# Depthwise convolution with 128-column stationaries and streams, and sample projections in four column quarters

## The chip, the cores and the metric

The kernel runs on one core of one Trainium2 chip. A core has TensorE (PE; its loads of stationary operands are PEld), VectorE (DVE), ScalarE (ACT), GpSimd (POOL), and SyncE (SP), which here issues most DMAs. Each runs its own list of instructions in order, and they meet at semaphores. The metric is the device time of one execution in microseconds (us). All data is float32. In the trace each float32 matmul shows as two records, and each transpose as one.

## The reference, cut to what matters

One decoder layer for 2048 prompt tokens and 8 sample tokens (one new token of each of 8 sequences). A projection of width 1792 is split into attention (512 query, 128 key, 128 value columns) and a convolution branch (512 value and 512 gate columns):

```python
proj = einsum('btd,de->bte', x, w_in) + b_in
q, k, v, ca, cg = split(proj)
attn = windowed attention (128 keys) of q, k, v with sinks
u = ca * sigmoid(cg)
conv = silu(layer_norm(depthwise_causal_conv(u, conv_w) + conv_b))    # width 31, 512 channels
mix = concat([attn, conv]) @ w_out + b_out
h = layer_norm(ALPHA * x + mix)
y = layer_norm(ALPHA * h + hierarchical_moe(h))                       # 32 experts, top 2
```

## The kernel before

The program is staged as follows, with the times of the profile.

**Input of the convolution (to 217 us).** The 16 prompt tiles of 128 tokens (`CONV_IN`) are projected onto the 1024 columns of the convolution branch, most of them in pairs (`pair_in`), and last the sample (`sample_in`, tile `NT`). DVE adds the biases (`evict_pair`, `evict_in`), ACT takes the sigmoid, DVE multiplies (`gated_in`), and SP stores `u` to DRAM (`u_rows`). `gather_windows(t)` then loads the stored rows back as overlapping windows into `ug`: partitions hold 62 positions of each of two channel quarters (plus two rows of ones for the bias), and the free axis holds 64 windows by 256 channels, so that the 64 windows of one channel lie 256 elements apart. SP works through its list in order; the load of the next x tile (`load_xT(18)`, which waits for `sample_in`) stands ahead of the last `gather_windows`.

**Attention and convolution (217 to 579 us), `STEPS` = 19 steps.** `QKV_IN` has the sample first. In step s, PE projects q, k, v of tile s (`project_sample` in step 0, else `project_in` with line 740: 512 query columns, then 256 key and value columns), and does the scores, transposes (`flip`) and values of tile s - 2. The order inside a step is written out by hand: first part of a convolution chunk, transposes of q and k (`turn_qk`, lines 756 and 757), second value half, scores (line 762), projection of q, (sample's own attention pieces in steps 1 to 9), projection of k and v, `flip` of the first half (line 770), second part of the chunk, `values` of the first half (line 778), `flip` of the second half. `values` waits for ACT's copy of the first flip (`ptA_ev`, line 1204), and `turn_qk` of the next step for ACT's copy of the second flip (`ptB_ev`, line 1213).

The convolution is done as Toeplitz products in 16 chunks (`CHUNK_OF`: two in step 0, two in step 1, then one a step up to step 13). A chunk is 8 slots by 2 column halves; each matmul (line 793) has 126 partitions, a stationary of 64 columns (two channels by 32 positions) and a stream of the 64 windows. The halves `h` = 0 and 1 go to output partitions 0 to 63 and 64 to 127 of the one bank `M1`, and one ACT copy (line 1209) moves the chunk's 128 x 512 results to `conv_sb`. The tables `toe` have two buffers; SP loads the table of chunk c + 2 after chunk c is done (`load_toe`, line 433), in its list behind the load of x for step s + 2, which waits for the key and value projection of step s. When all chunks are done, `conv_sb` goes to DRAM.

The sample's rows are few (8), so its projections (`sample_in`, lines 694 and 695; `project_sample`, line 747; `project_out_sample`, line 861) use 8-column stationaries and put two column halves into output partitions 0 to 7 and 64 to 71 (`rows_at`), with streams of 512 (384 for q, k, v). DVE adds bias or x from those partitions; line 1346 is the last add of `evict_in`, which PE waits for ahead of step 0.

**Output projection, h, routing (579 to 890 us); experts (to 1320 us); final norm.** In step 17 `project_out_sample` stands between the scores and the first flip of the last tile. The first prompt tile's output projection (`project_out(1, 0)`, line 874) waits for DVE's add of the sample's result (line 1496), which needs x plus bias from POOL (`bias_x`, line 1883) after POOL has scaled the bias (line 1902). The sample's x is loaded by `load_x(0)` in step 17, ahead of `load_attn(1)` and `load_attn(2)` on SP.

## Time and profile before

| | |
|---|---|
| median of 3 runs | 1383.74 us (1380.58 to 1384.69) |
| the profiled execution's own time | 1386.9 us |
| its span, first to last instruction | 1385.0 us |
| PE busy | 1276.4 us (92%) |
| DVE, ACT, POOL busy | 734.4, 539.4, 472.4 us |
| mean granted PE clock | 0.971 of full speed |

PE's busy time is long, but the ends of its records are modelled and records overlap; the starts are what to read. An entry in square brackets in a timeline is idle time of the engine ahead of the row and what ended it. A row that covers several instructions (x16) gives the start of the first and the length up to the end of the last.

### The profile page before, as it was taken

The page shows a single profiled execution, that of the slowest core. Times are in us where ns is not written, and L with a number is a line of the kernel's source. Part 1 is how long each engine was busy: PE and PEld are TensorE (multiplying, and loading weights), DVE is VectorE, ACT ScalarE, POOL GpSimd, SP SyncE. Part 2 cuts the span into 40 slices and gives each one's busy share as a digit, 9 for nine tenths or more (in the row PEclk, how much of TensorE's full clock was granted, in tenths as well). Part 3 has the DMA queues.
Part 4 walks back from the last instruction along what each step waited for, and adds up shares of the span by engine and source line. Part 5 has one row for each costly group of instructions (what it writes and reads, how often), then busy time and mean ns, then how long its engine had stood idle before and what let it go on. Part 6 is the DMA issues. An engine that isn't in the chain of part 4 may idle for free.

```text
span 1385.0 us, 21099 instructions
## 1 busy us (share of the span) xinstructions
PE 1276.4 (92%) x5477; PEld 607.3 (44%) x5478; DVE 734.4 (53%) x2079; ACT 539.4 (39%) x881; POOL 472.4 (34%) x640
## 2 busy tenths in 40 slices
PE   8999999989999988799999999999999999999910
PEld 3434444657666655355545555433333333333300
DVE  2423333463655555568888997344444444444338
ACT  0000101333445343323333331266665666656544
POOL 5112210000000000355555563344666566666312
PEclk9999999999999999999999999999999999999965
DMA  6354533222112165256655552269989999999776
GB/s 260 106 198 157 178 119 111 77 92 77 65 50 77 61 208 165 89 210 225 220 199 178 166 153 77 72 183 318 318 261 369 355 283 316 332 365 368 208 245 277
DMA packets 89957, 269.70 MB, mean 195 GB/s; under 512 B 14496, under 2 KB 40672, under 8 KB 76742
## 3 DMA queue, kind: packets, MB, share of 16 engines
q1 hardware_dynamic: 72903, 223.90, 45.2%
q0 software_dynamic: 14144, 41.26, 12.4%
q10 hardware_dynamic: 2823, 3.54, 0.8%
q8 instruction: 35, 0.57, 0.2%
q14 instruction: 52, 0.43, 0.1%
HBM read 209.66 MB, written 63.25 MB: 197 GB/s over the span
## 4 chain that ended last, share of the span: by engine, by line
PE 49%; issue 29%; DVE 9%; DMA 5%; DVEq 4%; ACT 1%; POOL 1%; SPq 1%; POOLq 1%; ACTq 0%
PE P L1032 13%; PE bank_S L1054 10%; PE M L1032 6%; PE bank_S L701 4%; PE P L701 3%; PE bank_T L701 2%; PE P L904 2%; PE bank_S L874 2%; DMA work<-conv_rows 2%; DVEq L1577 2%; PE M L701 2%; DVE route L1582 1%; PE M L1040 1%; DMA big<-sum_rows 1%; DVE work L1539 1%
## 5 line engine op out<-in xcount | busy, mean ns | idle before, releaser
L1272 ACT ACTIVATE big<-big 128x2048 f32 x78 | 148.9, 1910 | 155.4 <-issue 113.3
L1032 PE MATMUL P<-big,work 128*64 x416 | 188.0, 595 | 1.8 <-DVE work L1759 1.6
L1033 PE MATMUL P<-big,work 128*64 128x512 f32 x416 | 188.0, 595 | 0.0
L740 PE MATMUL P<-big,work 128*128 128x256 f32 (+1 forms) x512 | 173.6, 496 | 0.0
L1928 POOL DMA_INDIRECT work<-h_rows,piece_idx x152 | 145.8, 959 | 72.1 <-issue 51.4
L1054 PE MATMUL bank_S<-big,work 128*64 x312 | 140.4, 593 | 2.5 <-issue 1.5
L1056 PE MATMUL bank_S<-big,work 128*64 128x512 f32 x312 | 140.4, 593 | 0.0
L1865 POOL TENSOR_SCALAR work<-work 128x1 f32<-128x1 f32 (+1 forms) x17 | 3.8, 221 | 376.7 <-DVE work L1465 376.7
L740 PEld LDWEIGHTS P<-big,work 128*128 128x128 f32 x512 | 97.3, 194 | 70.4 <-issue 63.6
L874 PE MATMUL P<-big,work 128*128 128x512 f32 x256 | 113.8, 597 | 3.5 <-DVE work L1496 3.5
L874 PE MATMUL bank_S<-big,work 128*128 128x512 f32 x256 | 115.5, 605 | 0.0
L1032 PEld LDWEIGHTS P<-big,work 128*64 128x64 f32 x416 | 54.8, 137 | 108.7 <-issue 105.8
L1032 PE MATMUL M<-big,work 128*64 x208 | 94.2, 595 | 0.0
L1033 PE MATMUL M<-big,work 128*64 128x512 f32 x208 | 94.2, 595 | 0.0
L1746 DVE COPY work<-M 128x256 f32<-128x256 f32 x39 | 16.6, 425 | 125.3 <-PE M L1040 96.8
L1054 PEld LDWEIGHTS bank_S<-big,work 128*64 128x64 f32 x312 | 42.5, 137 | 91.7 <-issue 91.6
L1278 ACT ACTIVATE big<-big 128x2048 f32 x39 | 74.4, 1907 | 14.3 <-issue 13.7
L1101 ACT ACTIVATE work<-work 128x512 f32<-128x512 f32 (+1 forms) x17 | 10.7, 630 | 176.5 <-DVE work L1365 134.5
L1113 ACT ACTIVATE work<-work 128x256 f32<-128x256 f32 x128 | 63.4, 496 | 40.4 <-DVE work L1402 40.4
L1733 DVE STREAM_TRANSPOSE work<-work 128x1024 f32<-128x1024 f32 x38 | 77.7, 2045 | 0.3 <-issue 0.2
L874 PEld LDWEIGHTS P<-big,work 128*128 128x128 f32 x256 | 47.4, 190 | 57.3 <-issue 53.6
L874 PEld LDWEIGHTS bank_S<-big,work 128*128 128x128 f32 x256 | 48.0, 192 | 54.8 <-issue 54.7
(310 smaller groups left out, 2274.6 us busy)
## 6 DMA issues: line engine op xcount, KB each, us to landing
big<-in_w SPq DMA_DIRECT2D x96, 1024.0 KB
work<-in_xt_prompt SPq DMA_DIRECT2D x32, 512.0 KB, 3.5
big<-sum_rows SPq DMA_DIRECT2D x16, 520.0 KB, 8.9
big<-in_toe SPq DMA_DIRECT2D x16, 512.0 KB, 3.3
work<-in_x_prompt SPq DMA_DIRECT2D x16, 512.0 KB, 4.0
h_rows<-work SPq DMA_DIRECT2D x16, 512.0 KB
sum_rows<-work SPq DMA_DIRECT2D x16, 512.0 KB
out_y_prompt<-big SPq DMA_DIRECT2D x16, 512.0 KB
```

The costliest lines, as they stand in the source:

```text
L701: last = mm(dst, lhs[:, k, :], rhs[:, k, :], start=(first and k == 0), stop=(final and k == KD // 2 - 1), skip_group_check=not first)
L740: last = mm(dst[0:n, 0:c1 - c0], lhs[:, k, :], w_qkv[:, k, c0:c1], start=(k == 0), stop=(k == KD - 1))
L874: last = mm(OUT[c][half][0:n, :], lhs[:, k, :], w_out[:, k, half * 512:(half + 1) * 512], start=(k == 0), stop=(k == KD - 1))
L1032: mm(lower, xgT[j][:, k, 0:U], both[:, k], start=(k == 0), stop=(k == KD - 1))
L1033: last = mm(upper, xgT[j][:, k, U:P], w_up[:, k], start=(k == 0), stop=(k == KD - 1))
L1054: mm(bank_S[0:U, cols], gT[:, k, 0:U], wmem[:, bass.ds(off + 2 * KD * FF + k * D + half * 512, 512)], start=(k == 0), stop=(k == 1))
L1056: last = mm(bank_S[U:P, cols], gT[:, k, U:P], w_dn[side][:, k, cols], start=(k == 0), stop=(k == 1))
L1113: fn(smx[:, i, :], smx[:, i, :], ACT.Exp, bias=nm[:, c0 + i:c0 + i + 1], scale=SCALE, accum_out=rs[:, c0 + i:c0 + i + 1])
L1272: fn(w_up.rearrange("p k m f -> p m k f")[:, :, ks, :], src, ACT.Copy).then_inc(s[f"wu{part}_ok"], 1)
L1278: fn(dn_copy[b % 2], wmem[:, bass.ds(off + 2 * KD * FF, 2 * D)], ACT.Copy).then_inc(s["wd_ok"], 1)
L1733: nc.vector.transpose(xgT[j].rearrange("p k (i t) -> p i k t", i=4), xg[j].rearrange("p (i f k) -> p i k f", i=4, k=KD)).then_inc(s["xgT_e ...
L1928: g.indirect_dma_start(xg[j][:, 256 * i:256 * (i + 1)], None, h_pieces, bass.IndirectOffsetOnAxis(ap=piece_idx[:, j, i // 2, i % 2:i % 2 + ...
```

## The change

Four things change together.

1. The convolution's matmuls take both column halves at once: stationary of 128 columns (`h`, channel, position), stream of 128 columns (`h`, window). Half of the 128 x 128 output is used. Eight matmuls a chunk take the place of sixteen. Half a chunk (4 matmuls, `conv_part(chunk, part)`) now fills a bank of 512 columns; the first four half chunks go to four different banks (`CONV_FIRST`), all later ones to `M1`.
2. ACT evicts half a chunk at a time (`evict_conv`), in two copies of 64 partitions by 256 elements; `pe_cv` and `cv_ev` count half chunks.
3. The order in steps 0 and 1 differs: in step 1 the first part of chunk 2 stands ahead of the query projection, its second part behind it, the first part of chunk 3 behind the sample's piece, its second part at the end.
4. The sample's three projections use four column quarters at output partitions 0, 32, 64 and 96 (`quarter_rows`), with streams of 256 (192 for q, k, v), and DVE's adds and the load of the sample's x are split accordingly.

```diff
@@ helpers
+        ug_pairs = ug.rearrange("p w (h n) -> p h w n", h=2)
+        CONV_FIRST = [M1[:, :], bank_S[:, 0:512], bank_S[:, 512:], bank_T[:, 0:512]]
+        def conv_bank(n):
+            return CONV_FIRST[n] if n < len(CONV_FIRST) else M1[:, :]
-        def rows_at(tile, side):
-            at = side * HD if tile == NT else 0
-            return slice(at, at + rows_of(tile))
+        def quarter_rows(q):
+            return slice(32 * q, 32 * q + DEC)
@@ SP
             def load_toe(chunk):
-                after(sp, s["pe_cv"], chunk - 2)
+                after(sp, s["pe_cv"], chunk - 2, per=2)
...
                 if tile == NT:
-                    for half in range(2):
-                        cols = slice(512 * half, 512 * (half + 1))
-                        sp.dma_start(xb[0][rows_at(NT, half), cols], a["x_sample"][:, cols]).then_inc(s["xr_in0"], 16)
+                    for q in range(4):
+                        cols = slice(256 * q, 256 * (q + 1))
+                        sp.dma_start(xb[0][quarter_rows(q), cols], a["x_sample"][:, cols]).then_inc(s["xr_in0"], 16)
@@ PE: sample_in
-                    mm(CA[0][0:n, :], lhs[:, k, :], (B11 if low else B21)[:, kk, :], start=(k == 0), stop=(k == KD - 1))
-                    last = mm(CG[0][rows_at(NT, 1), :], (x_neg if low else x_sum)[:, kk, :], (T3 if low else B22)[:, kk, :],
-                              start=(k == 0), stop=(k == KD - 1))
+                    value = (lhs[:, k, :], (B11 if low else B21)[:, kk, :])
+                    gate = ((x_neg if low else x_sum)[:, kk, :], (T3 if low else B22)[:, kk, :])
+                    for q in range(4):
+                        bank, (tokens, weights) = ((CA[0], value), (CG[0], gate))[q // 2]
+                        cols = slice(256 * (q % 2), 256 * (q % 2 + 1))
+                        last = mm(bank[quarter_rows(q), cols], tokens, weights[:, cols], start=(k == 0), stop=(k == KD - 1))
@@ PE: project_sample (project_out_sample likewise, with 256 columns of w_out)
-                    for side, bank in enumerate((P0, P1)):
-                        last = mm(bank[rows_at(NT, side), 0:QKV // 2], lhs[:, k, :],
-                                  w_qkv[:, k, side * QKV // 2:(side + 1) * QKV // 2], start=(k == 0), stop=(k == KD - 1))
+                    for q in range(4):
+                        last = mm((P0, P1)[q // 2][quarter_rows(q), 0:QKV // 4], lhs[:, k, :],
+                                  w_qkv[:, k, q * QKV // 4:(q + 1) * QKV // 4], start=(k == 0), stop=(k == KD - 1))
@@ PE: the convolution
             def conv_part(chunk, part):
+                n = 2 * chunk + part
+                if n == 0:
+                    pe.wait_ge(s["ug_in"], 16 * 4 * NT)
                 if part == 0:
-                    if chunk == 0:
-                        pe.wait_ge(s["ug_in"], 16 * 4 * NT)
-                        after(pe, s["c_ev"], NT)
                     pe.wait_ge(s[f"toe_in{chunk % 2}"], 16 * (chunk // 2 + 1))
-                    after(pe, s["cv_ev"], chunk - 1)
-                for slot in range(4 * part, 4 * part + 4):
-                    for h in range(2):
-                        channel = h * P + chunk * 8 + slot
-                        last = mm(M1[h * 64:(h + 1) * 64, slot * 64:(slot + 1) * 64],
-                                  toe[chunk % 2][0:2 * SPAN + 2, slot, h, :], ug[0:2 * SPAN + 2, :, channel],
-                                  start=True, stop=True)
-                if part == 1:
-                    last.then_inc(s["pe_cv"], 1)
+                if n >= len(CONV_FIRST):
+                    after(pe, s["cv_ev"], n - 1)
+                for i in range(4):
+                    slot = 4 * part + i
+                    last = mm(conv_bank(n)[:, i * P:(i + 1) * P], toe[chunk % 2][0:2 * SPAN + 2, slot].rearrange("p h m -> p (h m)"),
+                              ug_pairs[0:2 * SPAN + 2, :, :, chunk * 8 + slot], start=True, stop=True)
+                last.then_inc(s["pe_cv"], 1)
@@ PE: order in the step loop
                 elif I:
                     pe.wait_ge(*x_landed(load))
                     after(pe, s["q_ev"], step - 1)
+                    if step == 1:
+                        conv_part(chunks[0], 0)
                     project_in(P0, load, 0, AD, s["pe_q"])
+                    if step == 1:
+                        conv_part(chunks[0], 1)
...
                 if step == 1:
-                    conv_part(chunks[0], 0)
-                    conv_part(chunks[0], 1)
+                    conv_part(chunks[1], 0)
...
-                if step <= 1:
+                if step == 0:
                     conv_part(chunks[1], 0)
+                    conv_part(chunks[1], 1)
+                elif step == 1:
                     conv_part(chunks[1], 1)
@@ ACT
+            def evict_conv(n):
+                at = n // 2 * 8 + n % 2 * 4
+                after(act, s["pe_cv"], n)
+                for h in range(2):
+                    rows = slice(64 * h, 64 * (h + 1))
+                    got = conv_bank(n)[rows, :].rearrange("p (n h w) -> p w h n", n=4, h=2)[:, :, h, :]
+                    last = fn(conv_sb[rows, :, at:at + 4], got, ACT.Copy)
+                last.then_inc(s["cv_ev"], 1)
...
+                if step >= 2 and CHUNK_OF[step]:
+                    evict_conv(2 * CHUNK_OF[step][0])
...
-                for chunk in CHUNK_OF[step]:
-                    after(act, s["pe_cv"], chunk)
-                    fn(conv_sb[:, :, chunk * 8:chunk * 8 + 8], M1[:, :].rearrange("p (j w) -> p w j", j=8),
-                       ACT.Copy).then_inc(s["cv_ev"], 1)
+                if step == 0:
+                    for n in range(4):
+                        evict_conv(n)
+                elif step == 1:
+                    evict_conv(2 * CHUNK_OF[1][1])
+                    evict_conv(2 * CHUNK_OF[1][1] + 1)
+                elif CHUNK_OF[step]:
+                    evict_conv(2 * CHUNK_OF[step][0] + 1)
@@ DVE: the sample's first add (those of q, k, v and of the output projection likewise)
+            def evict_sample():
+                b = NT % 2
+                after(v, s["pe_x"], NT)
+                for q in (2, 3):
+                    rows, cols = quarter_rows(q), slice(256 * (q - 2), 256 * (q - 1))
+                    tt(cgb[b][0:DEC, cols], CG[b][rows, cols], b_conv[rows, 256 * q:256 * (q + 1)], ALU.add)
+                after(v, s["u_st"], NT - 2, per=16)
+                for q in (0, 1):
+                    rows, cols = quarter_rows(q), slice(256 * q, 256 * (q + 1))
+                    last = tt(u[b][0:DEC, cols], CA[b][rows, cols], b_conv[rows, cols], ALU.add)
+                last.then_inc(s["c_ev"], 1)
```

## Rows read from the trace of the kernel before

**Rows 1.** Windows, 257 to 500 us: busy us (count) by engine, granted clock, DMA

```profile
257.00:500.00 243.00, 237.38 (x1416) 155.96 (x1415) 129.72 (x546) 105.00 (x298) 1.46 (x4) 0.99 0.20 68
```

**Rows 2.** Instructions of lines 694 and 695: ns min/median/max, first and last start

```profile
L694 PE MATMUL P<-big,work x16: 592/592/597, 210.6 to 217.0; 128*8 128x512 f32 x16
...
L695 PE MATMUL P<-big,smp x16: 592/592/596, 210.6 to 217.0; 128*8 128x512 f32 x16
```

**Rows 3.** Timeline, 357 to 363 us: start, length, engine, line, shape

```profile
357.73 1.36 PE L793 MATMUL M<-big 126*64 126x64 f32 x16
357.83 1.07 ACT L1204 ACTIVATE work<-bank_T 128x1024 f32<-128x1024 f32 x1 [3.74 <-PE bank_T L770]
...
358.96 1.08 PE L778 MATMUL M<-work 128*64 128x256 f32 x8
...
359.97 1.09 PE L770 MATMUL bank_S<-const,work 128*128 128x128 f32 x8
...
361.10 1.03 ACT L1213 ACTIVATE work<-bank_S 128x1024 f32<-128x1024 f32 x1 [1.36 <-PE bank_S L770]
...
362.28 0.65 PE L756 MATMUL bank_S<-const,work 128*128 128x128 f32 x4
```

**Rows 4.** Timeline, 557 us, a step without convolution work

```profile
557.40 1.08 PE L778 MATMUL M<-work 128*64 128x256 f32 x8 [1.12 <-ACT work L1204]
```

**Rows 5.** Timeline of PE at 238 us and at 596 us

```profile
238.23 0.41 PE L807 MATMUL M<-const,work 8*128 8x8 f32 x4
238.50 0.39 PE L809 MATMUL M<-const,work 8*128 8x8 f32 x4
...
596.11 1.04 PE L883 MATMUL bank_T<-const,work 8*128 8x8 f32 x8
597.08 0.70 PE L874 MATMUL bank_S<-big,work 128*128 128x512 f32 x1
```

**Rows 6.** Timeline, 214 to 231 us, with the DMA queue of SP

```profile
214.58 0.39 SPq L477 DMA_DIRECT2D u_rows<-work  x1
...
219.27 5.33 PE L747 MATMUL P<-big,work 128*8 128x384 f32 x32 [1.68 <-DVE work L1346]
219.41 0.44 SPq L428 DMA_DIRECT2D big<-u_rows  x1
...
224.53 2.55 PE L793 MATMUL M<-big 126*64 126x64 f32 x32
...
230.30 7.13 PE L740 MATMUL P<-big,work 128*128 128x512 f32 x16
```

**Rows 7.** DMA issues, 195 to 240 us: KB each, median us to landing

```profile
big<-in_toe SPq DMA_DIRECT2D x4, 512.0 KB, 3.3
...
big<-u_rows SPq DMA_DIRECT2D x6, 120.0 KB, 3.8
u_rows<-work SPq DMA_DIRECT2D x2, 256.0 KB, 2.4
```

**Rows 8.** Timeline of PE, 245 to 251 us

```profile
245.96 2.53 PE L793 MATMUL M<-big 126*64 126x64 f32 x32
250.99 1.22 PE L793 MATMUL M<-big 126*64 126x64 f32 x14 [2.50 <-DMA big<-in_toe]
```

**Rows 9.** Timeline of PE at 309 us, and window from 309 to 314.5 us

```profile
308.93 0.34 PE L831 MATMUL M<-const,smp 64*128 64x64 f32 x1 [3.74 <-DVE smp L1454]
...
309.00:314.50 5.50, 5.50 (x14) 4.30 (x15) 1.25 (x5) 0.22 (x1) 0.00 (x0) 0.50 0.00 0
```

**Rows 10.** Timeline, 568 to 580 us, the last attention step

```profile
568.53 1.14 DVE L1412 TENSOR_SCALAR work<-work 128x256 f32<-128x256 f32 x4
...
571.29 1.09 PE L770 MATMUL bank_T<-const,work 128*128 128x128 f32 x8
...
574.64 2.35 POOL L1883 TENSOR_TENSOR work<-work,lnx 128x1024 f32<-128x1024 f32 x1
...
579.11 7.13 PE L874 MATMUL P<-big,work 128*128 128x512 f32 x16 [3.50 <-DVE work L1496]
```

More of the change, by code:

```diff
@@ L859, in project_out_sample @@
                 for k in range(KD):
-                    for half in range(2):
-                        last = mm(OUT[c][half][rows_at(NT, half), :], mix_sT[:, k, :], w_out[:, k, half * 512:(half + 1) * 512],
+                    for q in range(4):
+                        at = 256 * (q % 2)
+                        last = mm(OUT[c][q // 2][quarter_rows(q), at:at + 256], mix_sT[:, k, :], w_out[:, k, 256 * q:256 * (q + 1)],
                                   start=(k == 0), stop=(k == KD - 1))
@@ L964, in _ @@
                 if step == NT + 1:
-                    after(pe, s["cv_ev"], CHUNKS - 1)
+                    after(pe, s["cv_ev"], 2 * CHUNKS - 1)
                     turn_z(1)
@@ L1195, in _ @@
                     exps(smB, G, s["nmB_ok"], s["expB_ok"], t)
+                if step == 1:
+                    evict_conv(2 * CHUNK_OF[1][0])
+                    evict_conv(2 * CHUNK_OF[1][0] + 1)
                 if 1 <= step <= 6:
@@ L1494, in add_half @@
                     after(v, s[f"pe_o{half}"], c - 1 + half)
-                rows = rows_at(OUT_IN[c], half)
-                stt(r[b][0:n, cols], xb[b][rows, cols], ALPHA, OUT[c][half][rows, :], ALU.mult, ALU.add
-                    ).then_inc(s[f"o{half}_ev"], 1)
+                if OUT_IN[c] < NT:
+                    last = stt(r[b][0:n, cols], xb[b][0:n, cols], ALPHA, OUT[c][half][0:n, :], ALU.mult, ALU.add)
+                else:
+                    for q in (2 * half, 2 * half + 1):
+                        rows, at = quarter_rows(q), 256 * (q % 2)
+                        cols = slice(256 * q, 256 * (q + 1))
+                        last = stt(r[b][0:n, cols], xb[b][rows, cols], ALPHA, OUT[c][half][rows, at:at + 256], ALU.mult, ALU.add)
+                last.then_inc(s[f"o{half}_ev"], 1)
             def norm_h(c):
@@ L1599, in _ @@
                         after(v, s["pe_x"], NT + 1)
-                        half, side = QKV // 2, rows_at(NT, 1)
-                        tt(qk[0:n, 0:half], P0[0:n, 0:half], b_qkv[0:n, 0:half], ALU.add)
-                        tt(qk[0:n, half:], P1[side, 0:AD + KVD - half], b_qkv[side, half:AD + KVD], ALU.add).then_inc(s["q_ev"], 1)
+                        part = QKV // 4
+                        for q in range(4):
+                            rows, lo, hi = quarter_rows(q), q * part, min((q + 1) * part, AD + KVD)
+                            last = tt(qk[0:n, lo:hi], (P0, P1)[q // 2][rows, 0:hi - lo], b_qkv[rows, lo:hi], ALU.add)
+                        last.then_inc(s["q_ev"], 1)
                     else:
@@ L1628, in _ @@
                     if tile == NT:
-                        tt(v_s[0:n, :], P1[side, 2 * KVD:QKV // 2], b_qkv[side, AD + KVD:], ALU.add).then_inc(s["kv_ev"], 1)
+                        rows = quarter_rows(3)
+                        tt(v_s[0:n, :], P1[rows, part - KVD:part], b_qkv[rows, AD + KVD:], ALU.add).then_inc(s["kv_ev"], 1)
                     else:
```

15 lines of the change are left out of this document (7 added, 8 removed).

## The prediction

> **What bounds the kernel now.** I read first the share of busy time by engine over the page, then the waits of the stage that the change touches (205 to 600 us), then the timeline of one of its steps. TensorE (PE below) is busy 237.38 of 243 us between 257 and 500 us [rows 1]. That looks as if each shorter matmul would shorten the span. The timeline says otherwise for the convolution. In a middle step half a chunk starts at 357.73, after the transposes of the first score half; ScalarE (ACT) copies those transposes from 357.83 to 358.90, and the value matmuls that need the copy start at 358.96, 0.06 after it. The other half chunk stands before 362.28: ACT's second copy ends at 362.13, and the transposes of queries start 0.15 later [rows 3]. In a step that has no convolution PE stands idle 1.12 us at this place, released by the same copy [rows 4]. So in the 12 steps with one chunk each, 24 half chunks lie in a hole that ACT's copies make, and they just fill it. What sets the end there is the chain flip, copy, values, flip, copy. Only in steps 0 and 1 (the first four chunks), in the sample's projections and in the last attention step can this change gain time.
>
> **The convolution in the middle steps.** Before, half a chunk is 16 records of 64 columns; two, one for each column half, run together. 32 records take 2.55 us [rows 6], 16 take 1.36 [rows 3]: (2.55 - 1.36) / 8 = 0.15 us for two together, 8 x 0.15 = 1.2 us for half a chunk. After, it is 8 records with 128 columns in both operands. No row shows this shape with these addresses, so I bound it. Lower end: 8 transposes of 128x128 take 1.09 us in all, 0.12 to 0.14 each [rows 3]. 8 x 0.12 = 0.95 us. The time between 0.95 and the 1.1 to 1.2 us of the hole is not gained, for the copy is still waited for: 24 x 0 = 0. Middle: the pair takes 0.15 us where 64 packed columns would take 64/512 of 0.43 us = 0.05 (15 distances between 210.6 and 217.0 [rows 2]). Something holds these streams back, and what sets them apart from all other streams is that they read every 256th element. If both halves share that limit, one stream of 128 elements reads as many elements as the two streams of 64 did: 0.15 again, 1.2 us, still in the hole. Upper end: the limit is each stream's own; then 128 elements cost twice 0.15 = 0.30, half a chunk 2.4 us. Transposes show how much a stride alone does: four loads of 128 packed columns go by in 0.27 us (0.07 each), eight of strided ones in 0.97 (0.12 each) [rows 5]. So strided reading runs at about 0.12 us for 128 elements when one stream is alone. That row is nearest to the new shape, and I take 0.12 to 0.15, which costs nothing in these steps, and keep 0.30 for the range.
>
> The Trainium skill ("SBUF — State Buffer", section "Door 1: The DMA port swizzle") says that memory is read in lines of 16 bytes, and that each access which goes to a new line pays. Both the slow pairs and the strided transposes agree with it, and it speaks against this change if every stream pays for itself; by it alone the sum would be the second rival below.
>
> **ACT's copies.** One copy of 512 columns a chunk becomes four of 64 partitions by 256. Bounds: a quarter of the 1.07 us for 1024 columns [rows 3], 0.27, and half of it, 0.53. I take 0.4, so 0.8 for half a chunk. The later one falls between 358.90 and 361.10, where ACT stands idle for 2.2 us [rows 3]; the earlier one ahead of the exponentials, which wait for VectorE. Cost nothing; if that cover went, 0.8 us a step, 10 us in all.
>
> **Sample's projections.** Four streams of half the length in four column quarters take the place of two. First projection: 16 distances of 0.43 [rows 2] = 6.9 us become 3.4 if four run together; the second 5.26 (219.27 to 224.53 [rows 6]) becomes 2.6; output projection like the first, 6.9 to 3.4. No row has four together. Bounds: all of that, or nothing. I take all, since two together cost no more than one does. The Trainium skill ("TensorE: Matmul & The Clock Gate", "Part 3: Packing small matmuls — row/col tiling") reports 2.38 times for three column tiles; at that rate the gain would be a little under mine. VectorE's adds become four of 256 instead of two of 512; the wait of 1.68 us [rows 6] that holds them grows by 0 to 0.6, I take 0.3.
>
> **What of it arrives in steps 0 and 1.** The first projection ends 3.4 us earlier, at 214.0. PE waits 1.9 for the adds and starts the second at 215.9, done at 218.5. Then the convolution needs the windows of the last prompt tile. Their store is issued at 214.58 and takes about 2.4 to 2.8, so the window loads can't leave before 217.3. Their four issues span 1.4 us; the last was issued at 219.41 and landed 3.8 later, at 223.2, just ahead of PE's 224.53 [rows 6, 7]. Now: 217.3 + 1.4 + 3.8 = 222.5. Of 6.0 us only 224.5 - 222.5 = 2.0 arrive; the rest becomes PE's wait.
> Four half chunks (four banks, no eviction between them) take 4 x 1.2 = 4.8, to 227.3. The next half chunk stands ahead of step 1's projection. It needs the filter table of chunk 2, a load that SP issues once chunk 0 is done (224.9) and that lands 3.3 after its issue [rows 7]: 228.3. ACT's last copy for the banks is done by then (227.3 + 0.9). The half chunk is done at 229.5, and the projection starts there instead of at 230.30 [rows 6]: 0.8 gained. With 0.12 a record: 222.5 + 3.8 = 226.3; table 222.5 + 1.9 + 3.4 = 227.8; projection at 228.8: 1.5 gained, and 0.5 more from two half chunks before the end of step 1. That end (keys and values) was 245.96. From there x for step 3 and the table of chunk 4 are loaded, and PE goes on at 250.99, 5.0 later [rows 8]. The load is triggered by that same projection, so step 2 starts 0.8 to 2.0 earlier, whatever PE saves behind it. Its wait for the table grows, since only half a chunk stands in it: from 2.50 to 5.0 - 1.2 = 3.8 us.
> That has a price. After the wait of 3.74 us at 308.93 the granted clock was 0.50 (1.2 GHz) for 309.0 to 314.5, which cost half of 5.5, 2.75 us [rows 9]. After 3.8 us the same can come: bounds 0 and 2.75, I take 1. (PE's other long wait, 218.5 to 222.5, has the table's wait behind it, which swallows most of what a slow clock costs there.)
>
> **The last step.** The output projection ends 3.4 earlier, but the flip behind it needs VectorE's scaling, which ends at 569.67: flip at 569.8 instead of 571.29, 1.5 gained. The tail then begins with an add that needs GpSimd's x plus bias, ready at 576.99, behind a weight load that does not move; the projection of tile 0 can't start before about 577.8 instead of 579.11: 1.3 [rows 10]. The sample's x comes in four DMAs instead of two, about 1 us more on SP ahead of two loads that PE needs at 577.8; covered.
>
> **Sum.** -0.8 to -2.0 (head), 0 (middle), -1.3 (last step), +1 (clock): -1.1 to -2.3, say -1.7. The profiled execution took 1386.9 (span 1385.0), 3.2 over the median of 1383.74; from the median, 1382.0. A run of this kernel can tell 0.3%, 4.15 us: no change.
>
> **Rivals.** (1) Likeliest, as above: 0.44. Within 0.3% in 0.38, faster in 0.06, should the window loads come sooner and the clock hold.
> (2) Slower: the strided limit is each stream's own. Place: the 24 half chunks in the hole. It decides from 1.25 us / 8 = 0.16 us a record. At 0.22, half a chunk takes 1.76: 24 x 0.55 = 13 us, the head turns to about +3, the last step stays: +15, 1399. At 0.30: 24 x 1.2 = 29, head +7, 1419. For it: the pair's 0.15. Against it: the lone strided load at 0.12 [rows 5]. 0.31.
> (3) Faster: PE's time counts in full, as its busy share suggests [rows 1]. Then 3.4 + 2.6 + 3.4 for the sample and 32 x 0.25 for the convolution, 17 us: 1366. Half of it, if DMAs follow sooner than I think: 1375. Against it: the copies end 0.06 ahead of the values [rows 3]. 0.18.
> (4) The quarters don't run together: sample unchanged, last step 0, and the half chunk ahead of step 1 waits for its table until 230.8, 1.7 later than now: 1385. 0.07, same.
>
> Faster 0.06 + 0.18 = 0.24, same 0.38 + 0.07 = 0.45, slower 0.31. Range: from 1376 (half of rival 3 left out) up to 1402 (the upper part of rival 2 left out); the likeliest case's own is 1378 to 1386.
>
> **What would show it.** Records of the convolution at 0.12 to 0.15 us, values still 0.06 us behind ACT's copy, steps of unchanged length; PE idle about 4 us ahead of the first half chunk for the window loads, and 3.8 us or more ahead of chunk 4; the output projection 3.4 us long and the tail's first projection 1.3 us nearer to it. Records above 0.16 us would make the prediction wrong, and so would window loads that land well before 222 us.

## The result, and the profile after

| | median us | runs | ratio to before, 95% interval |
|---|---|---|---|
| before | 1382.16 (1379.64 to 1384.69) | 4 | |
| after | 1394.53 (1394.33 to 1398.54) | 4 | 1.0095 (1.0075 to 1.0115) |

The change costs 12.4 us; I had forecast no change (1382.0). The time lies inside the range, near what rival 2 gives for 0.22 us a record (1399). That it comes so near is in part luck: of rival 2's terms the hole turned out smaller (10 us for 13) and the head larger (8.4 for 3), as shown below.

The timeline of one middle step after the change, which answers to [rows 3]:

```profile
365.31 1.04 PE L778 MATMUL bank_T<-const,work 128*128 128x128 f32 x8
366.19 1.92 PE L801 MATMUL M<-big 126*128 126x128 f32 x8
366.39 1.02 ACT L1230 ACTIVATE work<-bank_T 128x1024 f32<-128x1024 f32 x1 [3.74 <-PE bank_T L778]
368.03 1.08 PE L786 MATMUL M<-work 128*64 128x256 f32 x8
368.14 0.77 ACT L1128 ACTIVATE big<-M 64x256 f32<-64x256 f32 x2 [0.73 <-PE M L801]
369.05 1.09 PE L778 MATMUL bank_S<-const,work 128*128 128x128 f32 x8
369.98 1.92 PE L801 MATMUL M<-big 126*128 126x128 f32 x8
370.18 1.02 ACT L1243 ACTIVATE work<-bank_S 128x1024 f32<-128x1024 f32 x1 [1.27 <-PE bank_S L778]
371.72 0.62 PE L764 MATMUL bank_S<-const,work 128*128 128x128 f32 x4
```

ACT's first copy ends at 366.39 + 1.02 = 367.41, and the values start at 368.03, 0.62 behind it; before it was 0.06. The second ends at 371.20, and the transposes of queries start 0.52 behind it; before 0.15. No wait stands in brackets at either, for PE no longer waits for the copy: it is still busy with the convolution. The hole has become too short for what lies in it.

All instructions of that half chunk, with the times of the first and the last start:

```profile
L801 PE MATMUL M<-big x8: 382/397/397, 366.2 to 367.7; 126*128 126x128 f32 x8
```

Seven distances in 1.5 us: 0.22 us a record (218 to 220 ns in the raw starts), where I had taken 0.12 to 0.15.

The head, timeline of PE, against [rows 6, 8]:

```profile
214.69 2.79 PE L755 MATMUL P<-big,work 128*8 128x192 f32 x64 [2.04 <-DVE work L1386]
221.05 2.00 PE L801 MATMUL M<-big 126*128 126x128 f32 x8 [3.57 <-DMA big<-u_rows]
...
229.27 1.97 PE L801 MATMUL M<-big 126*128 126x128 f32 x8 [0.95 <-ACT big L1128]
231.06 8.74 PE L748 MATMUL P<-big,work 128*128 128x512 f32 x16
...
249.10 1.91 PE L801 MATMUL M<-big 126*128 126x128 f32 x8
254.51 2.00 PE L801 MATMUL M<-big 126*128 126x128 f32 x8 [3.49 <-DMA big<-in_toe]
...
258.43 2.08 PE L770 MATMUL bank_S<-work 64*128 64x256 f32 x8 [0.85 <-ACT work L1209]
```

Step 2 starts at 254.51 where it started at 250.99. Eight records of the scores take 2.08 us, where they took 1.13 before. The windows say why (their last three columns are granted clock, DMA share and GB/s), first before, then after:

```profile
205.00:300.00 95.00, 88.51 (x572) 53.83 (x571) 42.68 (x150) 26.75 (x73) 0.00 (x0) 1.00 0.34 111
```

```profile
205.00:300.00 95.00, 83.42 (x480) 56.92 (x479) 40.90 (x141) 28.85 (x85) 0.00 (x0) 0.93 0.27 87
```

In this stretch the clock was 1.00 before; after, it is at 0.50 (the lower of its two levels) for 3.41 us from 221.2, 3.41 from 231.4 and 6.83 from 255.3.

The end of the attention steps, PE, against [rows 10]:

```profile
580.63 3.64 PE L868 MATMUL P<-big,smp 128*8 128x256 f32 x64
586.04 1.09 PE L778 MATMUL bank_T<-const,work 128*128 128x128 f32 x8 [1.77 <-DVE work L1453]
...
594.44 9.92 PE L881 MATMUL P<-big,work 128*128 128x512 f32 x16 [4.08 <-DVE work L1542]
```

### The profile page after: what moved, and what is told of

It is laid out like the page before. It is cut to its first block, busy times and chain, and to the rows that moved or that the text cites. A ratio compares the mean times of both kernels' runs of the same rounds, so it can differ in the third digit from the quotient of the medians.

```text
span 1396.6 us, 20834 instructions
## 1 busy us (share of the span) xinstructions
PE 1284.6 (92%) x5317; PEld 626.0 (45%) x5318; DVE 735.0 (53%) x2085; ACT 553.0 (40%) x929; POOL 473.6 (34%) x640
## 4 chain that ended last, share of the span: by engine, by line
PE 47%; issue 30%; DVE 10%; DVEq 5%; DMA 4%; ACT 1%; POOL 1%; POOLq 1%; SPq 1%; ACTq 0%
PE P L1044 13%; PE bank_S L1066 9%; PE M L1044 6%; PE bank_S L709 4%; PE P L709 3%; DVEq L1623 3%; PE bank_T L709 2%; PE P L911 2%; DVE route L1628 2%; PE M L709 2%; PE M L1052 1%; PE bank_S L881 1%; DVE work L1585 1%; DMA work<-conv_rows 1%; DMA big<-sum_rows 1%
## 5 line engine op out<-in xcount | busy, mean ns | idle before, releaser
L881 PE MATMUL P<-big,work 128*128 128x512 f32 x256 | 116.6, 609 | 4.1 <-DVE work L1542 4.1
```

The source lines that it names most:

```text
L881: last = mm(OUT[c][half][0:n, :], lhs[:, k, :], w_out[:, k, half * 512:(half + 1) * 512], start=(k == 0), stop=(k == KD - 1))
```

## The experiments

Medians in us; the kernel before was run beside each, and the ratio is to it. For all kernels with a profile I also read three stretches of PE's starts: the **head** (first start of `sample_in` to the first values of step 2), the **middle** (first values of step 4 to those of step 14, nine chunks) and the **end** (from there to the first `project_out`):

```
                        median   ratio, 95% interval        head   middle  end
before                  1382.2                              59.96  198.49  63.03
after                   1394.53  1.0095 (1.0075 to 1.0115)  68.34  206.12  63.38
packed_stream           1382.03  1.0005 (0.9981 to 1.0028)  61.59  197.76  62.62
pairs_in_new_order      1383.97  1.0014 (0.9993 to 1.0035)  64.15  198.49  65.18
quarters_only           1379.28  0.9985 (0.9965 to 1.0004)  59.42  198.49  66.21
conv_only               1396.54  1.0115 (1.0071 to 1.0159)  70.29  206.12  64.59
neighbours              1381.54  0.9995 (0.9975 to 1.0015)  63.55  197.75  62.79
pairs_short_head        1379.03  0.9982 (0.9962 to 1.0002)  57.80  198.50  65.82
neighbours_short_head   1380.50  0.9989 (0.9971 to 1.0006)  57.29  197.75  63.09
neighbours_in_holes     1394.37  1.0091 (1.0071 to 1.0111)  62.09  207.24  67.33
keys_in_hole            1376.56  0.9970 (0.9953 to 0.9986)  63.03  194.74  63.01
both_in_holes           1368.75  0.9909 (0.9880 to 0.9938)  57.74  189.39  63.47
pairs_both_in_holes     1382.23  1.0001 (0.9979 to 1.0023)  58.68  199.92  63.45
before_filled           1389.56  1.0060 (1.0039 to 1.0082)  70.55  198.48  66.28
quarters_filled         1382.62  1.0008 (0.9994 to 1.0023)  66.66  198.53  65.59
after_filled            1397.99  1.0126 (1.0100 to 1.0152)  71.48  206.12  64.29
quarters_filled_less    1376.56  0.9956 (0.9939 to 0.9974)  59.65  198.48  65.62
both_in_holes_filled    1361.65  0.9851 (0.9828 to 0.9874)  56.88  189.39  63.60
```

The middle repeats to 0.05 us wherever the same matmuls stand in it. Head and end come from one profiled execution each, and they change with the granted clock. The stages behind them, whose work the change leaves as it is, took 798 to 806 us in these profiles, a spread of the size of the effects looked for. The kernel before itself had medians of 1381.5 to 1383.6 in the sets that were run beside the others, so a difference of two medians of different sets holds up to 2 us of that; the ratios don't.

### Taking the change apart

**The stream's addresses alone.**

```diff
-                              ug_pairs[0:2 * SPAN + 2, :, :, chunk * 8 + slot], start=True, stop=True)
+                              ug_flat[0:2 * SPAN + 2, P * (chunk * 8 + slot):P * (chunk * 8 + slot + 1)], start=True, stop=True)
```

> The changed kernel with one thing altered: each of the convolution's 128-column streams reads 128 neighbouring elements instead of 128 elements that lie 256 (and 128) apart. Number, size, order and waits of all matmuls stay; the values that come out of the convolution are not the reference's. Theory 1 (the stride sets the price, and the price of each stream is its own): a record falls from 0.22 us to what a 128x128 transpose takes, 0.11, half a chunk from 1.92 to about 1.0 us, the value matmuls stand 0.06 us behind ACT's copy again, and the time falls by 24 x 0.45 = 11 us, to 1381 to 1386. Rival (the 128-column stationary, the half banks or the new order cost the time): a record stays at 0.22 or the steps stay as long as they are, 1392 to 1397.

1382.03. In its timeline the half chunk is short, and PE waits for ACT's copy at both places:

```profile
356.01 1.06 PE L801 MATMUL M<-big 126*128 126x128 f32 x8
356.21 1.02 ACT L1230 ACTIVATE work<-bank_T 128x1024 f32<-128x1024 f32 x1 [3.74 <-PE bank_T L778]
...
357.28 1.08 PE L786 MATMUL M<-work 128*64 128x256 f32 x8 [0.22 <-ACT work L1230]
...
359.23 1.06 PE L801 MATMUL M<-big 126*128 126x128 f32 x8
359.43 1.02 ACT L1243 ACTIVATE work<-bank_S 128x1024 f32<-128x1024 f32 x1 [1.55 <-PE bank_S L778]
...
360.60 0.63 PE L764 MATMUL bank_S<-const,work 128*128 128x128 f32 x4 [0.31 <-ACT work L1243]
```

Same shape, same stationaries, same order: only the distance of the elements differs. The middle falls from 206.12 to 197.76, and that is just 0.7 below the pairs of before: a half chunk of 0.9 us gains next to nothing over one of 1.2 to 1.3, as the prediction had it.

**The old pairs in everything else that is new.**

```diff
-                    last = mm(conv_bank(n)[:, i * P:(i + 1) * P], toe[chunk % 2][0:2 * SPAN + 2, slot].rearrange("p h m -> p (h m)"),
-                              ug_pairs[0:2 * SPAN + 2, :, :, chunk * 8 + slot], start=True, stop=True)
+                    for h in range(2):
+                        last = mm(conv_bank(n)[h * 64:(h + 1) * 64, i * P + h * 64:i * P + (h + 1) * 64], toe[chunk % 2][0:2 * SPAN + 2, slot, h, :],
+                                  ug[0:2 * SPAN + 2, :, h * P + chunk * 8 + slot], start=True, stop=True)
```

> The changed kernel with the old matmul form alone: pairs of 64-column stationaries and 64-window streams, written into the new half banks, in the new order, evicted half a chunk at a time, with the sample's quarters. Theory 1 (the form of the stream alone costs the time): a pair is back at 0.15 us, half a chunk at 1.2 to 1.36, the waits behind ACT's copies at 0.06 and 0.15, and head and last step keep what the quarters gave: 1377 to 1383, so 3 us or more under the kernel before. Rival (order, half evictions or the clock in the head cost it): 1388 to 1395.

1383.97, and the middle is 198.49 again: ACT's half evictions cost nothing there. But against the quarters alone the head is 4.7 us longer (64.15 against 59.42). Step 2 starts 41.72 us behind the first projection instead of 39.30, which is 2.4 of it. The other 2.3 lie inside step 2, where this execution had a clock of 0.50 for 10.24 us and that of the quarters for 3.41. So the stream cost the middle, and the new order with its clock the head.

**The sample's quarters alone** (the parts of the diff that name `quarter_rows` and `evict_sample`), and **the convolution's part alone** (the rest).

> The kernel before with the sample's three projections in four column quarters (and VectorE's adds and the x loads split with them), the convolution untouched. Theory 1 (my steps for head and last step hold): the first projection takes 3.5 us instead of 6.9, but steps 1 and 2 start only 1 to 2 us earlier, since windows and tables are waited for, and the last step gives 1.3: 2 to 3.5 us faster than before. Rival (the time saved on TensorE comes through in full): 8 to 9 us faster. Second rival (the last step's projection waits for VectorE anyway and the split x loads delay the tail): no difference.

1379.28: 3.4 us below the median before, though the interval just holds 1. The head gives 0.5, not the 1 to 2 forecast: step 2 starts 1.1 us sooner, and 0.6 of that goes to a clock of 0.50 for 3.41 us in step 2, which the kernel before didn't have.

> The kernel before with all of the convolution's part of the change (128-column matmuls, half banks, new order, half evictions) and the sample's projections in two halves as before. Theory 1: the middle steps lose 24 x 0.45 = 11 us as in the changed kernel, and the head and last step don't get what the quarters gave: 12 to 17 us slower than before, 1395 to 1400. Rival (the quarters themselves cost time somewhere, for instance by the clock drops ahead of step 2 that the changed kernel shows): less than 10 us slower than before, 1386 to 1392.

1396.54, 13.9 slower, as expected. The quarters give back about 2 of it, less than four runs of each can tell.

### What a stream costs

> A measurement of records, not of the time. The changed kernel with another stream in each chunk of the convolution; its values are not the reference's. One 128-column stationary with 128 elements at a distance of 1 (chunk 4), 2 (5), 4 (6), 8 (7), 16 (8), 64 (9) elements, with runs of 2 (10) and of 4 (11) neighbours every 256 elements; one 64-column stationary alone with 64 elements 128 apart (12); pairs of them in both column halves at distances 1 (13), 4 (14), 64 (15). Theory 1 (each element from another 16-byte line costs a stream its own 1.72 ns): 0.11 us at a distance of 1, about 0.11 to 0.15 at 2, 0.22 from 4 on, 0.11 to 0.15 for the runs; the lone stream of 64 takes 0.11, and a pair 0.144 at 4 and 64 and 0.055 to 0.07 at 1. Rival (the price grows with the distance, for instance only from some hundred bytes on): 0.11 at 4 and 8 and 0.22 only at 64. Second rival (both halves of a pair share one limit): the lone stream of 64 takes half of what a pair takes, 0.07.

The records are what counts here, not the time (one run, 1410.7 us, of which 16 us or more above the other kernels lie behind the attention steps). First and last start of a half chunk give seven distances. Chunk 4 (distance 1, its second half), 5 (2), 6 (4), 7 (8), 9 (64), 10 (runs of 2), 11 (runs of 4):

```profile
L817 PE MATMUL M<-big x8: 273/275/275, 271.6 to 272.4; 126*128 126x128 f32 x8
...
L817 PE MATMUL M<-big x8: 273/274/280, 274.8 to 275.6; 126*128 126x128 f32 x8
...
L817 PE MATMUL M<-big x8: 391/405/406, 318.8 to 320.3; 126*128 126x128 f32 x8
...
L817 PE MATMUL M<-big x8: 394/412/414, 322.6 to 324.2; 126*128 126x128 f32 x8
...
L817 PE MATMUL M<-big x8: 383/397/397, 382.5 to 384.1; 126*128 126x128 f32 x8
...
L817 PE MATMUL M<-big x8: 271/272/277, 402.6 to 403.4; 126*128 126x128 f32 x8
...
L817 PE MATMUL M<-big x8: 273/275/275, 405.8 to 406.6; 126*128 126x128 f32 x8
```

0.8 / 7 = 0.11 us up to a distance of 2 elements and with runs of 2 or 4; 0.22 to 0.23 from a distance of 4 on, whether 16 bytes or 256 (chunk 8, with 64 bytes, 0.22 too). It is a step, not a slope. The 64-column forms, lone with a distance of 128 (chunk 12), and pairs at 1, 4 and 64 (chunks 13 to 15):

```profile
L820 PE MATMUL M<-big x8: 287/288/306, 426.0 to 426.8; 126*64 126x64 f32 x8
...
L820 PE MATMUL M<-big x16: 222/222/270, 445.5 to 445.9; 126*64 126x64 f32 x16
...
L820 PE MATMUL M<-big x16: 294/296/310, 465.0 to 465.8; 126*64 126x64 f32 x16
...
L820 PE MATMUL M<-big x16: 322/334/336, 484.5 to 485.5; 126*64 126x64 f32 x16
```

The lone stream of 64 takes 0.11, a pair 0.06, 0.12 and 0.14. So a scattered element costs its stream 1.7 ns, a packed one 0.9, and two streams in two column halves pay side by side, nearly as if each were alone. The change put the 128 elements of a pair into one stream, where they pay one after the other: theory 1, and both rivals fall.

The Trainium skill ("SBUF — State Buffer", section "Door 1: The DMA port swizzle") says that a 16-byte line wants at least two hits to be read at full rate. By that rule, the trace agrees: distance 2 and runs of 2 are free, distance 4 is not. The page also calls a stride of 4 fp32 elements free; here it took 0.23 us against 0.11, and the measurement decides.

**The same form, with neighbours.** Stationaries take channels 2k and 2k + 1, and the tables, gains and output weights are laid out to fit:

```diff
-                              ug_pairs[0:2 * SPAN + 2, :, :, chunk * 8 + slot], start=True, stop=True)
+                              ug[0:2 * SPAN + 2, :, 2 * (chunk * 8 + slot):2 * (chunk * 8 + slot) + 2], start=True, stop=True)
```

> The changed kernel with its 128-column form, order and evictions, but with channels 2k and 2k + 1 as the two halves of a stationary in place of k and k + 128, so that the stream reads runs of 2 neighbouring elements every 256; tables, gains and output weights are laid out to fit, and the result is the reference's. Theory 1 (what costs is that each element lies in another 16-byte line): a record takes 0.112 us as in the run with runs of 2, half a chunk 0.9, and the time is that of the packed stream, 1380 to 1385, 10 to 13 us under the changed kernel. Rival (something in the real data path, for instance the eviction that now reads every second element, takes the gain back): 1387 or more.

1381.54, 13.0 us below the changed kernel, with the middle at 197.75 and this record of a half chunk:

```profile
L801 PE MATMUL M<-big x8: 271/272/275, 356.6 to 357.4; 126*128 126x128 f32 x8
```

### The order of step 1

```diff
-                    if step == 1:
-                        conv_part(chunks[0], 0)
                     project_in(P0, load, 0, AD, s["pe_q"])
                     if step == 1:
-                        conv_part(chunks[0], 1)
+                        conv_part(chunks[0], 0)
...
                 if step == 1:
-                    conv_part(chunks[1], 0)
+                    conv_part(chunks[0], 1)
...
                 elif step == 1:
+                    conv_part(chunks[1], 0)
                     conv_part(chunks[1], 1)
```

> The new half banks, evictions and quarters with the old pairs, and step 1 in another order: query projection, first part of chunk 2, the sample's piece, second part of chunk 2, keys and values, both parts of chunk 3. So no table is waited for ahead of the query projection, and two half chunks instead of three stand ahead of the keys and values, whose end triggers the loads for step 2. Theory O (the new order of step 1 costs 3 to 5 us by the table's wait ahead of the projection and the later trigger): 1378 to 1381, like the quarters alone. Rival (the half evictions cost it): 1383 to 1385, as with the pairs in the new order.

> Runs of 2 neighbours and this other order of step 1. Theory O with theory 1: 2 to 3 us under the neighbours in the new order and not more than 1 or 2 under the quarters alone, for the middle steps wait for ACT's copies: 1377 to 1380. Rival (PE's 0.4 us a half chunk count in full): 24 x 0.4 = 10 us under the quarters alone, 1369.

1379.03 and 1380.50. The heads fall from 64.15 to 57.80 and from 63.55 to 57.29, some 6 us, of which 1 (neighbours) to 5 us (pairs) show in the medians. Step 2 starts 3.5 us sooner in both, 38.27 instead of 41.72 us behind the first projection with pairs. The other 3 us lie in step 2, where the clock was at 0.50 for 10.24 and 6.83 us with the new order and never with the short head. Whether the order brings that is open: `keys_in_hole` below has the short head and a drop of 10.24 us in step 2, and its head is 63.03. Neither beats the quarters alone by anything that can be told; PE's cheaper half chunks don't count in full.

### Is a middle step bound by its holes?

A hole is the stretch from the end of a flip to the end of ACT's copy of it; half a chunk of the convolution stands in it, and PE waits for what is left. With neighbours and the short head, these waits between 262 and 520 us (line waited, in all, times, longest) were:

```profile
PE bank_S L764 <- ACT work L1245: 5.8, 13, 1.2
PE M L786 <- ACT work L1232: 3.7, 13, 1.1
```

> As the kernel before it in this list, and one of the eight steps of the key and value projection (two records of 256 columns, 0.43 us) moved from ahead of the first flip to the place behind the convolution in each of ACT's two copies, in steps 2 to 13; two steps of it at each place in steps 14 to 16. Theory H (what bounds a middle step is work outside the holes plus the holes, so only work moved into them counts): each hole gives back what is waited there now, 0.22 and 0.31 us in 12 steps and about 0.9 twice in three: 6.4 + 5 = 11 us, 1367 to 1371. Rival (VectorE, which gets keys and values later, or the loads behind the projection are late next): 1376 or more.

1394.37: the rival, and more. The longest of PE's waits in the same stretch:

```profile
PE bank_S L774 <- DVE work L1483: 19.8, 12, 1.6
```

The transposes of queries wait for VectorE's rotation of keys, which can't begin before the keys' last matmul, now behind the second hole. So only the first hole may take a part of the keys (the first addition below, behind the second convolution part); the second hole takes the first step of the queries (the second addition, behind the first part), and in `keys_in_hole` nothing.

```diff
+                if late(step):
+                    project_part(P1, load, AD, QKV, KD - late(step), KD, s["pe_x"])
...
+                if 3 <= step <= NT:
+                    pe.wait_ge(*x_landed(load))
+                    after(pe, s["q_ev"], step - 1)
+                    project_part(P0, load, 0, AD, 0, 1, s["pe_q"])
```

> Runs of 2 neighbours, the short head, and the last step of the key and value projection (0.43 us; two steps in steps 14 to 16) moved only into the first hole, behind the second convolution part. VectorE then has keys and values 3.3 us sooner than with a step in both holes, ahead of the place where the transposes of queries wait for it (1.65 us there). Theory H (work moved into a hole counts with what is waited there): 12 x 0.22 + 3 x 0.87 = 5 us under the same kernel without the move (1380.5), 1373 to 1377. Rival (the later keys and values hold VectorE and through it the next step): no gain or slower, 1380 or more.

> As before it in this list, and in the second hole, behind the first convolution part, the first step of the query projection (two records of 512, 0.87 us), in steps 3 to 16. It is longer than the 0.31 us waited there, so the transposes of queries come 0.55 later, but it is 0.87 less ahead of the first flip. Theory H: another 12 x 0.31 + 3 x 0.87 = 6 us, 1367 to 1371. Rival (scores come later, so the softmax ends later, and the first flip waits for VectorE): no further gain, or up to 15 x 0.5 = 8 us lost, above all in steps 14 to 16, where the flip waits for VectorE already.

> The kernel with work in both holes (last step of keys and values in the first, first step of the queries in the second) and the short head, but with the old pairs of 64-column matmuls. Theory H: in steps 2 to 13 a half chunk of pairs fills its hole, nothing is waited there, and moved work changes nothing; only steps 14 to 16 give back up to 3 x 1.7 = 5 us against the pairs with the short head alone (1379.0): 1374 to 1378, and the cheap streams are worth the other 6 to 8 us. Rival (the move itself gains, whatever the streams cost, for instance by a better order for VectorE): 1368 to 1371, as with neighbours.

1376.56 (middle 194.74) and 1368.75 with neighbours, both as theory H had it. With pairs 1382.23, where I had expected 1374 to 1378: the end is 2.4 us shorter than without the moves, but the head 0.9 and the middle 1.4 longer. A middle step of the second kernel's timeline has no wait left:

```profile
347.14 1.04 PE L788 MATMUL bank_T<-const,work 128*128 128x128 f32 x8
348.01 1.06 PE L811 MATMUL M<-big 126*128 126x128 f32 x8
348.91 0.59 PE L757 MATMUL P<-big,work 128*128 128x256 f32 x2
349.43 1.08 PE L796 MATMUL M<-work 128*64 128x256 f32 x8
350.45 1.09 PE L788 MATMUL bank_S<-const,work 128*128 128x128 f32 x8
351.38 1.06 PE L811 MATMUL M<-big 126*128 126x128 f32 x8
352.28 1.02 PE L757 MATMUL P<-big,work 128*128 128x512 f32 x2
353.14 0.60 PE L774 MATMUL bank_S<-const,work 128*128 128x128 f32 x4
```

The middle is 189.39, 8.4 below the same streams without the moves (197.75); with pairs the same moves give 199.92, 1.4 above 198.50. The hole is the bound: it was full with pairs, so cheap streams are worth nothing until other work moves in (1379.03 with pairs, 1380.50 with neighbours), and moved work is worth nothing until the streams are cheap (1379.03 without, 1382.23 with, which the runs can't tell apart). Together they are worth 1379.03 - 1368.75 = 10.3 us.

### What the slow clock costs

The waits of the head and the tail were filled with matmuls without use:

```diff
+                if step == 2:
+                    after(pe, s["cv_ev"], 3)
+                    fill(M1, 5)
```

> The kernel before with the sample's quarters, and matmuls without use (512 columns, the identity against a constant) in four of TensorE's waits: 9 ahead of the first convolution part, 5 ahead of the convolution of step 2 (table), 7 ahead of the sample's transpose in step 4 (its softmax), 7 ahead of the first output projection. Theory C (the clock falls behind a long wait, and its time is lost on the path): no drop of the granted clock behind these four waits, 1.7 us back for each drop of 3.41 us and 3.4 for each of 6.83: 5 to 9 us faster than the kernel before, 1374 to 1378. Rival (the slow stretches are swallowed by later waits, or the fillers push the work behind them): within 2 us of the quarters alone, 1378 to 1382.

> The kernel before with the same four fillings and nothing else. Theory C: only the drop behind the 3.74 us wait at 308 us is there to be avoided, 2 to 3.4 us faster than before; the filling ahead of the first part finds no wait and costs up to 3.9 us, of which the table's wait swallows 2.5. Sum: -2 to +1 against before. Rival (waits don't move the clock): +1 to +4.

> The changed kernel with the same four fillings. If the clock drops of the head and the tail are a part of the 12 us that the change cost, they come back here: 5 to 8 us under the changed kernel, 1386 to 1390, and 24 x 0.45 = 11 us of the middle steps stay. Rival (the middle steps are all of it): 1392 to 1396.

The medians are 3.3, 7.4 and 3.5 us above those of the same kernels without, and only the second stands clear of the intervals. The mistake was mine: a matmul of 512 columns is two records, 0.86 us, so nine take 7.8 us in a wait of 4.3 (from the start of `sample_in` to the first convolution part: 18.00 us against 12.73). These three say nothing on the clock. With 4, 2, 3 and 4:

> The kernel before with the sample's quarters and fillings that fit into the waits: a matmul of 512 columns takes 0.86 us (two records), so the first fillings (9, 5, 7, 7) were about twice as long as the waits that they stood in. Now 4, 2, 3 and 4 of them, 3.4, 1.7, 2.6 and 3.4 us. Theory C (a slow clock behind these waits is paid on the path): the drops at 220, 248, 306 and 579 us are gone or shorter and the time falls by 1.7 to 3.4 us for each, 4 to 8 in all, against the quarters alone (1379.3): 1371 to 1375. Rival (what the slow clock costs is swallowed by the waits behind it): 1378 to 1381.

> The fastest kernel so far (runs of 2 neighbours, short head, work in both holes) with the same shorter fillings. Theory C: 3 to 7 us under 1368.75, 1362 to 1366. Rival (swallowed, or the waits here are shorter than the fillings): 1367 to 1371.

1376.56 and 1361.65: 2.7 and 7.1 us below the same kernels without fillings, where I had expected 4 to 8 and 3 to 7. The intervals of the first two ratios (0.9965 to 1.0004, 0.9939 to 0.9974) overlap, those of the second two don't. The windows from 205 to 320 us of the quarters alone, first without, then with fillings:

```profile
205.00:320.00 115.00, 100.07 (x727) 66.38 (x727) 52.24 (x189) 34.02 (x94) 0.00 (x0) 0.94 0.29 96
```

```profile
205.00:320.00 115.00, 107.46 (x763) 68.85 (x762) 53.43 (x203) 35.63 (x99) 0.00 (x0) 1.00 0.29 95
```

The clock is 1.00 throughout, and the stretch from the values of step 2 to those of step 4, where the drop behind the wait for the sample's softmax stood [rows 9], falls from 47.22 to 44.27. In the fastest kernel that stretch falls from 44.59 to 42.98, and one drop of 3.41 us stays ahead of step 2. So what the clock takes is in good part on the path. Behind the last filling, the time from the first start of `project_out` to its seventeenth falls from 12.77 to 10.04 and from 13.05 to 10.04. The two gains in the medians are known to within 4 and 5 us, by their intervals. The last kernel is the fastest of the study, 1.5% below the kernel before.

## Why the prediction was wrong

**The convolution in the middle steps: the failing step.** "That row is nearest to the new shape, and I take 0.12 to 0.15, which costs nothing in these steps": 0.22 was measured, above my own threshold of 0.16, and the sum's term for the middle, 0, came out as 7.6 us in nine chunks. The row was that of stationary loads [rows 5], and its absolute value was carried to streams. Its ratio was the thing to carry: scattered loads took 0.12 where packed ones took 0.07. Applied to a stream of 128 packed columns, 128/512 of 0.43 = 0.11, that gives about 0.2. (That loads and streams pay by the same ratio is how the numbers came out, not something that a run set out to test.) The pair's 0.15 [rows 3, 6] was also read as a limit shared by both halves, though it is close to one stream's 64 x 1.7 ns = 0.11, paid by both at the same time.

**The hole: right.** A shorter half chunk gained 0.7 us in nine chunks, and the longer one is paid. Only the size was off: rival 2 took 0.55 a half chunk, 24 of them 13 us; the middle grew by 206.12 - 198.49 = 7.63 us for 18 half chunks, 0.42 each, 10 for all 24. The second hole had 0.1 us more room, and the flips ahead of the convolution end 0.1 sooner.

**ACT's copies: right.** 0.77 for two against 0.8, hidden; with the old pairs the middle was the same 198.49.

**Sample's projections: right on TensorE.** The 32 instructions of each half start from 209.0 to 212.3, 16 rounds of four in 3.4 us, and the second projection takes 2.8 (2.6).

```profile
L704 PE MATMUL P<-big,work x32: 379/379/383, 209.0 to 212.3; 128*8 128x256 f32 x32
```

**Head: the wait was right, the order's price was missed.** The windows were waited for until 12.04 us behind the start of the first projection; forecast 222.5 - 210.55 = 11.95 (the other kernels with quarters and no fillings have 12.0 to 13.5, so the last digits are luck). But four half chunks took 7.3 us instead of 4.8, then came an eviction (0.95) that I had thought done, and the projection started at 231.06. Rival 2's head was +3; the trace has +8.4. The pairs' kernel splits that: 64.15 - 59.42 = 4.7 with the new order (three half chunks instead of two ahead of the keys' end, which triggers the loads of step 2), 68.34 - 64.15 = 4.2 with the streams, and -0.5 with the quarters. Half of the 4.7 is slow clock in step 2. Up to the start of step 2 alone I had forecast a gain of 0.8 to 2.0; behind the start of the first projection it stands at 40.44 before, 39.30 with the quarters, 41.72 with pairs in the new order and 45.50 after, so a loss of 1.3 with pairs and of 5.1 with the change.

**The clock: too small.** +1 was forecast. Three drops came in the head, 13.65 us at half speed. The first lay on scattered streams, which didn't slow down (last section). By the second the first query projection took 8.74 us instead of 7.13. In the third the query projection of step 2 started 262.14 - 254.51 = 7.6 us behind the step's first record, 255.83 - 250.99 = 4.8 before; 0.5 of the difference is the scattered half chunk. That makes some 4 us, an estimate from these starts. What a clock without drops would give back in the changed kernel itself was not measured, for its fillings were too long; in two others fillings of the right length were worth 2.7 and 7.1 us.

**Last step: right, and lost again.** The flip waits 1.77 for VectorE, as said, and `project_out` starts 13.81 us behind the sample's projection instead of 14.79: 1.0 gained (forecast 1.3). Then its first 16 records take 9.92 instead of 7.13, for the clock was at 0.50 from 593.3 on, for 6.83 us, and had fallen in the 4.08 us of wait ahead of it.

**Sum of the medians.** Quarters -3.4 (1382.68 to 1379.28), new order with half evictions +4.7 (to 1383.97), the stream +10.6 (to 1394.53): +11.9 of the 12.4 measured. Each of the three carries 3 to 4 us of uncertainty, by the intervals in the table.

## What to carry to other kernels

Look at how far apart the elements of a stream lie before merging or splitting matmuls. For float32 here, 128 elements took 0.11 us at distances of 1 and 2 and in runs of 2, and 0.22 from a distance of 4 on. Two streams in different column halves pay that at the same time, while one long stream pays it in a row. Where a matmul lies in a hole that another engine makes, its price matters only beyond the hole's length; a cheaper one is worth what you move in behind it, and what moves must be what nobody is waiting for. Of a neighbouring row carry the ratio between its two states, not its value.

## What the runs showed of the hardware that was not expected

- Scattered streams don't feel the lower clock. In the changed kernel records at 0.50 lay as far apart as at 1.00: 222.9 to 224.4 for eight. Packed ones in the ladder's chunks 0 and 1 at 0.50 took 3.2 us for 15 distances, 0.213 each, against 0.11. A scattered stream at full clock costs what a packed one costs at half.

```profile
221.30:224.50 3.20, 3.20 (x16) 3.20 (x16) 0.91 (x5) 0.76 (x2) 0.00 (x0) 0.50 0.25 93
...
L801 PE MATMUL bank_S<-big x8: 397/397/398, 222.9 to 224.4; 126*128 126x128 f32 x8
```

```profile
219.00:224.00 5.00, 5.00 (x24) 5.00 (x25) 0.34 (x2) 1.51 (x4) 0.00 (x0) 0.50 0.08 20
...
L817 PE MATMUL bank_S<-big x16: 421/421/421, 220.7 to 223.9; 126*128 126x128 f32 x16
```

- Four streams of 256 columns in four column groups go by in 0.215 us a round, one stream's time: 16 rounds, 3.4 us.
- Pairs whose elements lie 4 apart took 0.12, pairs at 64 apart 0.14 to 0.15. Why a pair pays a little more at large distances stays open.
